# Six of the twelve modulation chunks move from TensorE's four-strip sums to GpSimd and one-column matmuls

## The chip, the cores and the metric

One core of one Trainium2 chip runs the whole program in one launch. The metric is the device time of an execution in microseconds (us). Everything is float32.

## The reference, cut to what matters

One layer of a hybrid diffusion step for 512 sample tokens and 128 prompt tokens, model width 1024. The change touches only where and when the adaLN modulation is computed:

```
cond -> silu(cond) @ w_ada + b_ada            w_ada: 1024 x 6144, two conditions (c, c_ctx)
     -> sh1, sc1, g1, sh2, sc2, g2            six rows of 1024 for each condition
h = rmsnorm(x) * (1 + sc1) + sh1
y = concat(rglru(h ...), hgrn2(h ...)) @ w_out
x = x + g1 * y
h = rmsnorm(x) * (1 + sc2) + sh2
x = x + g2 * expert_choice_ffn(h)             16 experts, capacity 2T/16
```

sh1 and sc1 are wanted at the very start; g1, sh2, sc2 and g2 only after the mixer. A chunk is 512 of the 6144 columns: chunks 0 to 3 are sh1 and sc1 ("early"), chunks 4 to 11 the rest ("late").

## The kernel before, in words

All matrices pass through a ring of six slots in SBUF of 2 MB each (128 partitions, eight k tiles of 512 columns). SyncE issues the loads in the fixed order of LOADS (line 52); each waits until its slot is free (`freed[s]`). The eight late chunks all go through slot 4, one after the other, behind the first projection's weights; then slot 4 takes the weights of the gate projection. Behind them in the same queue stand w_out and the experts' weights (line 345).

Every engine runs an order written out by hand, and the engines meet at semaphores. TensorE's order in the middle of the program: four convolution inputs, the gates of the RG-LRU, five projections of head 0 (HEAD0), one projection taken ahead (EARLY), and then eight "units", one for each of four heads in two directions (line 709). A projection (lines 470 to 489) is eight matmuls of 512 sample columns and eight of 128 prompt columns into one of two PSUM buffers, pa[0] and pa[1], which ScalarE empties; USE numbers them. A unit has two or three projections (FILL) as filler between its own steps: turn v, turn k, the state updates, the scores (five blocks, each masked by VectorE; block n waits for the mask of block n-2), and the outputs. VectorE's side of a unit is: sums of log decays (line 1414), differences (line 1398), weighing of the operands (line 1394), then the state step (lines 1454 to 1463), which writes state_out, and after it the masks (line 1478) and the sum of the outputs.

A modulation chunk (ada_sum, line 491) is eight k steps of four matmuls that have two stationary columns (the two conditions) and 128 moving columns, each of the four in its own strip of 32 PSUM partitions. ScalarE copies two chunks' sums to SBUF, two transposes turn them (ada_turn), and VectorE adds the bias into `mods` (ada_bias). ADA_UNIT says where the pairs of late chunks stand: positions 4 and 5 in unit 0, 6 and 7 in unit 1, 8 and 9 in unit 3, 10 and 11 in unit 5.

GpSimd in this stage only issues DMAs, in order (lines 386 to 402). In unit u it waits for the outputs of unit u-2, loads the state of unit u into s0, then waits for the state step of unit u-1 and stores that state from state_out: the store in iteration u is that of unit u-1, and VectorE's state step of unit u waits for it (line 1457), because it writes the same state_out. Before unit 0 the queue waits for the last RG-LRU state (line 386) and for `lru_y` (line 391).

Of the kernel before, what the change touches and what calls it, by code (L numbers as in the profile page):

```python
# [80 lines left out]
ADA_UNIT = {0: 4, 1: 6, 3: 8, 5: 10}  # L81
# [3 lines left out]
def program(nc, x_prompt, x_sample, state_lru, state_hgrn, c, c_ctx, w_ada, b_ada, norm_mix, w_in,  # L85
# [7 lines left out]
    with ctx:  # L93
# [32 lines left out]
        ada_sb = sb("ada_sb", [P, 2 * P])  # L126
        eps = sb("eps", [P, 1])
# [112 lines left out]
        ada_zero, adr_ps, adr_done = sem("mod_sums_zeroed"), sem("mod_rows_in_psum"), sem("mod_rows_copied")  # L240
        ada_ps, ada_add, mods_done = sem("mods_turned"), sem("mods_added"), sem("mods_done")
# [14 lines left out]
        sp_done = sem("softplus_done")  # L256
# [103 lines left out]
        def _(pool):  # L360
# [24 lines left out]
            pool.dma_start(w_rt[:, :, :], w_router[0].rearrange("(k p) n -> p k n", p=P)).then_inc(s_wbd, 16)  # L385
            pool.wait_ge(lst_done, 1)
            pool.dma_start(flat(new_state_lru).rearrange("(r q) -> r q", q=P), lru_last_r[:, :]).then_inc(st_dma, 16)
            for u in range(2 * HEADS):
                h, d = u // 2, u % 2
                if u == 0:  # L390
                    pool.wait_ge(lru_y, 1)
                if u >= 2:
                    pool.wait_ge(o_ps, u - 1)
                pool.dma_start(s0[u % 2], state_hgrn[0, 0, d, h]).then_inc(s0_in[u % 2], 16)
                if u >= 1:
                    pool.wait_ge(s_done, u)
                    pool.dma_start(new_state_hgrn[0, 0, (u - 1) % 2, (u - 1) // 2], state_out[:, :]).then_inc(st_dma, 16)
                if u == UNITS - 1:
                    pool.wait_ge(rows_cp, 1)
                    pool.dma_start(mod_rows.rearrange("r (k q) -> (r k) q", q=P), row_turn[:, :]).then_inc(rows_st, 16)  # L400
# [54 lines left out]
        def _(pe):  # L455
# [21 lines left out]
            def project_prompt(item):  # L477
                g, j = item
                n, s = USE[item], SLOT_OF[("in", g)][0]
                for k in range(KT):  # L480
                    r = mm(pa[n % 2][:, TS:T], ring[:, s, k, j * P:(j + 1) * P], hT[:, k, TS:T], k == 0, k == KT - 1)
                r.then_inc(full, 1)
# [21 lines left out]
            def ada_turn(at):  # L504
                pe.wait_ge(adr_done, at // 2 + 1)
# [447 lines left out]
        def _(act):  # L953
# [28 lines left out]
            def ada_copy(at):  # L982
# [4 lines left out]
                if at >= 2:  # L987
                    act.wait_ge(ada_ps, at // 2)
# [39 lines left out]
            def lru_gates(j):  # L1028
# [9 lines left out]
                if j == 0:  # L1038
                    act.wait_ge(sp_done, 1)
# [19 lines left out]
            def projected(item):  # L1059
# [3 lines left out]
                src, e = pa[n % 2][:, 0:T], empty[n % 2]  # L1063
                if g == IN_OG:
# [159 lines left out]
        def _(dve):  # L1224
# [38 lines left out]
            def ada_bias(at):  # L1263
                dve.wait_ge(ada_ps, at // 2 + 1)
# [48 lines left out]
            V.tensor_scalar(sp[:, 3, :], acc8, 8.0, None, ALU.mult).then_inc(sp_done, 1)  # L1313
# [94 lines left out]
            for u in range(UNITS):  # L1408
# [42 lines left out]

                if u in ADA_UNIT:
# [221 lines left out]
```

## Time and profile before

| what | us |
|---|---|
| runs of the kernel before | 1067.31, 1068.09, 1062.74; median 1067.31 |
| the profiled execution | 1062.3 |
| its span, first to last instruction | 1060.6 |
| TensorE busy | 992.4 (94%) |
| VectorE busy | 353.8 (33%) |
| ScalarE busy | 288.6 (27%) |
| GpSimd busy | 87.5 (8%), DMA issues almost alone |
| mean granted TensorE clock | 0.98 |

In the rows further down, PE is TensorE, PEld its weight loads, DVE VectorE, ACT ScalarE, POOL GpSimd; SPq and POOLq are the DMA queues of SyncE and GpSimd. L457 is line 457 of the kernel, a helper through which nearly all matmuls pass, so the tiles tell which matmul it is: `ring,cs` is a modulation chunk, `reg_a,ring` a projection. A float32 matmul shows as two records. A timeline row gives its start, the time it covers, and in brackets how long the engine was idle before it and who ended that. The granted clock is 1.00 at TensorE's 2.4 GHz and 0.50 at 1.2 GHz.

### The profile page before, as it was taken

Reading aid. Unit: us, or ns where it says so; the run is one execution under the profiler, and the core shown is the slowest. Engines: PE = TensorE matmul, PEld = TensorE weight load, DVE = VectorE, ACT = ScalarE, POOL = GpSimd, SP = SyncE. Lnnn points to the kernel's source line nnn. Section 1 sums busy time; section 2 is a strip of 40 time slices with the busy share of each in tenths; the row PEclk is TensorE's granted clock in tenths of the full one; section 3 lists DMA queues with packets and bytes.
Section 4 is the critical chain, followed back from the end, with each engine's and each line's share of the span. In section 5 each row is a group of like instructions: output and inputs, shape, how many; then the busy total and the mean of one; then the engine's idle time right before and its main releaser. Section 6 shows DMA issues by size and latency. Waiting matters only on the chain.

```text
span 1060.6 us, 18108 instructions
## 1 busy us (share of the span) xinstructions
PE 992.4 (94%) x7918; PEld 451.8 (43%) x7918; DVE 353.8 (33%) x819; ACT 288.6 (27%) x445; POOL 87.5 (8%) x102
## 2 busy tenths in 40 slices
PE   4999999999999999993999999999999999999990
PEld 3555556666666765553233233333333333333230
DVE  2367726453642663455103021030210302103024
ACT  5147545563652554431100010000100001000012
POOL 2200000000000000000101102011020110201101
PEclk9999999999999999996999999999999999999995
DMA  9980013404028424215499999999999999999947
GB/s 352 353 292 0 1 39 132 164 6 159 6 85 300 185 87 174 80 60 198 159 410 395 399 409 392 404 395 401 410 392 404 393 404 410 393 403 393 404 192 223
DMA packets 82366, 277.26 MB, mean 261 GB/s; under 512 B 3889, under 2 KB 4065, under 8 KB 82321
## 3 DMA queue, kind: packets, MB, share of 16 engines
q1 hardware_dynamic: 74688, 253.24, 61.3%
q0 software_dynamic: 5392, 15.46, 5.3%
q10 hardware_dynamic: 2240, 7.91, 1.9%
q8 instruction: 34, 0.56, 0.2%
q14 instruction: 12, 0.09, 0.0%
HBM read 262.94 MB, written 13.65 MB: 261 GB/s over the span
## 4 chain that ended last, share of the span: by engine, by line
PE 73%; DMA 19%; DVE 4%; SPq 2%; ACT 1%; issue 1%; DVEq 0%; ACTq 0%
PE pa L457 49%; PE p L457 20%; DMA ring<-in_w_up_dram 15%; DMA ring<-in_w_ada_dram 3%; SPq L338 1%; PE p L877 1%; PE p L833 1%; DVE reg_e L1460 1%; DVE reg_a L1647 1%; DMA reg_c<-h_rows,row_s 1%; PE p L838 0%; PE p L594 0%; DMA sum_rows<-reg_c,row_b 0%; PE pa L932 0%; DMA sum_rows<-reg_c,row_s 0%
## 5 line engine op out<-in xcount | busy, mean ns | idle before, releaser
L457 PE MATMUL pa<-ring,reg_b 128*32 128x512 f32 (+1 forms) x3232 | 413.4, 595 | 2.9 <-DMA ring<-in_w_up_dram 2.9
L457 PEld LDWEIGHTS pa<-ring,reg_b 128*32 128x32 f32 (+1 forms) x3232 | 129.9, 114 | 257.3 <-issue 256.8
L457 PE MATMUL pa<-reg_a,ring 128*128 128x128 f32 (+1 forms) x832 | 232.4, 435 | 0.0
L457 PE MATMUL p<-ring,reg_b 128*16 128x512 f32 x1536 | 173.6, 593 | 0.0
L457 PEld LDWEIGHTS pa<-reg_a,ring 128*128 128x128 f32 x832 | 126.1, 191 | 93.6 <-issue 93.6
L963 ACT ACTIVATE reg_b<-pa 128x512 f32<-128x512 f32 (+1 forms) x28 | 17.1, 612 | 284.6 <-PE pa L457 228.7
L1617 DVE TENSOR_TENSOR reg_b<-reg_b,pa 128x512 f32<-128x512 f32 x16 | 11.0, 688 | 247.4 <-PE pa L457 247.4
L457 PEld LDWEIGHTS p<-ring,reg_b 128*16 128x16 f32 x1536 | 43.3, 97 | 112.2 <-issue 108.7
L963 ACT ACT_TABLE_LOAD x64 | 82.1, 1283 | 5.1 <-issue 2.8
L963 ACT ACTIVATE reg_b<-p 128x512 f32<-128x512 f32 x24 | 14.3, 597 | 196.1 <-PE p L877 169.8
L1585 DVE TENSOR_SCALAR reg_b<-p,ffn_scale,mods 128x128 f32<-128x128 f32 x72 | 23.8, 403 | 72.2 <-PE p L833 72.2
L963 ACT ACTIVATE reg_c<-reg_c 128x320 f32<-128x320 f32 (+1 forms) x86 | 43.3, 574 | 1.7 <-DVE reg_c L1377 0.7
L435 POOL DMA_INDIRECT sum_rows<-reg_c,row_s x8 | 11.8, 1471 | 346.5 <-DVE reg_c L1630 346.5
L457 PE MATMUL p<-reg_c 128*16 128x16 f32 (+3 forms) x640 | 36.4, 212 | 2.2 <-DVE reg_e L1478 1.4
L1394 DVE SCALAR_TENSOR_TENSOR reg_c<-reg_c,oml 128x320 f32<-128x320 f32 (+1 forms) x40 | 27.1, 681 | 20.5 <-ACT reg_c L963 20.5
L457 PE MATMUL p<-reg_c,reg_e 128*128 128x128 f32 (+1 forms) x128 | 31.2, 359 | 2.9 <-ACT reg_b L963 1.4
L963 ACT ACTIVATE reg_d<-pa 128x640 f32<-128x640 f32 (+2 forms) x24 | 15.6, 659 | 60.8 <-PE pa L457 60.7
L457 PEld LDWEIGHTS p<-reg_c 128*16 128x16 f32 (+3 forms) x640 | 27.3, 115 | 11.4 <-DVE reg_e L1478 3.0
L1637 DVE SCALAR_TENSOR_TENSOR reg_c<-p,slot_q,reg_c 16x512 f32<-16x512 f32 x32 | 23.9, 746 | 22.8 <-PE p L457 22.4
L1630 DVE SCALAR_TENSOR_TENSOR reg_c<-pa,slot_s,reg_c 128x512 f32<-128x512 f32 x16 | 12.0, 751 | 56.5 <-PE pa L457 56.5
L1398 DVE TENSOR_TENSOR reg_c<-reg_c 128x640 f32<-128x640 f32 x40 | 30.1, 820 | 0.3
L457 PE MATMUL p<-ring,cs 128*2 128x128 f32 x768 | 23.3, 274 | 1.9 <-DMA ring<-in_w_ada_dram 1.8
(248 smaller groups left out, 702.6 us busy)
## 6 DMA issues: line engine op xcount, KB each, us to landing
ring<-in_w_gate_dram SPq DMA_DIRECT2D x32, 2048.0 KB, 14.1
ring<-in_w_up_dram SPq DMA_DIRECT2D x32, 2048.0 KB, 19.0
ring<-in_w_down_dram SPq DMA_DIRECT2D x32, 2048.0 KB, 17.8
ring<-in_w_ada_dram SPq DMA_DIRECT2D x12, 2048.0 KB, 19.5
ring<-in_w_in_dram SPq DMA_DIRECT2D x7, 2048.0 KB, 20.0
ring<-in_w_out_dram SPq DMA_DIRECT2D x2, 2048.0 KB, 16.8
sum_rows<-reg_a ACTq DMA_DIRECT2D x5, 512.0 KB, 2.6
h_rows<-reg_d ACTq DMA_DIRECT2D x5, 512.0 KB, 2.7
```

Source lines behind the costliest of these rows:

```text
L338: sp_eng.dma_start(ring[:, s], src).then_inc(loaded[s], 16)
L435: pool.indirect_dma_start(sum_rows, bass.IndirectOffsetOnAxis(row_s[0:CS, i:i + 1], 0), out_s[0:CS, :], None, compute_op=ALU.add).then_inc ...
L457: return nc.tensor.matmul(out, lhsT, rhs, start=start, stop=stop, **kw)
L833: r = nc.tensor.transpose(p67[:, k * P:(k + 1) * P], xg_s[:, k * P:(k + 1) * P], ident[:, :])
L877: r = nc.tensor.transpose(p67[:, f * P:(f + 1) * P], hid_s[:, f * P:(f + 1) * P], ident[:, :])
L963: return nc.scalar.activation(out, in_, f, **kw)
L1394: return V.scalar_tensor_tensor(dst, src, s, dst, ALU.mult, ALU.mult)
L1398: V.tensor_tensor(dst.rearrange("p (g x) -> p g x", x=x), c3, c3[:, :, at:at + 1].to_broadcast([P, T // x, x]), ALU.subtract).then_inc(sub ...
L1585: r = V.tensor_scalar(xsT[:, k, :], p67[:, k * P:(k + 1) * P], ffn_scale[:, k, 0:1], mods[:, 3 * KT + k, 0:1], ALU.mult, ALU.add)
L1617: V.tensor_tensor(hv, hv, pa[1][:, cols_], ALU.mult).then_inc(hid_done, 1)
L1630: V.scalar_tensor_tensor(out_s[:, cols_], pa[1][:, cols_], slot_s[:, 1, bass.ds(i, 1)], g2r[0][:, cols_], ALU.mult, ALU.mult).then_inc(out ...
L1637: r = V.scalar_tensor_tensor(out_p[32 * e:32 * e + CP, cols_], p45[rs, 512:1024], slot_q[rs, bass.ds(i, 1)], g2r[1][rs, cols_], ALU.mult, ...
```

## The change

Late chunks 4 to 9 (by position) leave TensorE's four-strip sums. For each, GpSimd multiplies the eight k tiles by the condition's value of each partition and adds them up over k, for both conditions, into ada_part (two rows of 512 a partition); of the products, all but the first two are written over ring tiles that are used up. Then eight matmuls with 128 columns of ada_part as weights and one column of ones as the moving operand sum over partitions; they stand at the end of the prompt half of a given projection, and write eight columns of the same PSUM buffer behind it. ADA_AT says which projection: the third of HEAD0, EARLY, and the first fill of units 1, 2, 3 and 4. ScalarE copies the eight columns to ada_cols, and VectorE adds the bias in units 0 (two chunks), 1, 2, 3 and 4. On GpSimd chunks 4 and 5 stand ahead of the store of the last RG-LRU state, and chunks 6 to 9 in iterations 0 to 3 between the load of a state and the store of the last one. GpSimd frees slot 4. Chunks 10 and 11 stay as they were, in unit 5. The semaphore sp_done goes into sp_e.

```diff
--- before.py
+++ after.py
@@ -78,7 +78,13 @@
 N_USE = len(USE)
 UNITS = 2 * HEADS
 
-ADA_UNIT = {0: 4, 1: 6, 3: 8, 5: 10}
+
+ADA_AT = {HEAD0[2]: 4, EARLY: 5, FILL[1][0]: 6, FILL[2][0]: 7, FILL[3][0]: 8, FILL[4][0]: 9}
+
+ADA_UNIT = {5: 10}
+ADA_TURN = {0: 1, 2: 2, 10: 3}
+AT_ITEM = {at: item for item, at in ADA_AT.items()}
+
 Y_ORDER = [4, 5, 6, 0, 1, 2, 3, 7]
 
 
@@ -124,6 +130,8 @@
         ss_h = sb("ss_h", [P, 2, NT])
         z_rt = sb("z_rt", [P, 2, NE])
         ada_sb = sb("ada_sb", [P, 2 * P])
+        ada_part = sb("ada_part", [P, 2, 512])
+        ada_cols = sb("ada_cols", [P, 6, 8])
         eps = sb("eps", [P, 1])
         hn = sb("hn", [P, T])
         cs = sb("cs", [P, KT, 2])
@@ -238,6 +246,7 @@
         pe_cols, pv_done = sem("param_columns"), sem("param_columns_copied")
         cs_done = sem("cond_silu")
         ada_zero, adr_ps, adr_done = sem("mod_sums_zeroed"), sem("mod_rows_in_psum"), sem("mod_rows_copied")
+        part_done = sem("mod_parts_done")
         ada_ps, ada_add, mods_done = sem("mods_turned"), sem("mods_added"), sem("mods_done")
         rows_ps, rows_cp, rows_st = sem("mod_rows_turned"), sem("mod_rows_ready"), sem("mod_rows_stored")
         act_step, dve_step, pool_step = sem("act_step"), sem("dve_step"), sem("pool_step")
@@ -253,7 +262,6 @@
         lru_done, lsq_done = sem("lru_tile_done"), sem("lru_squares")
         ln_ps, ln_log, ln_rstd, lru_y, gr_y = sem("lru_norm_sums"), sem("lru_norm_log"), sem("lru_norm_rstd"), sem("lru_y_done"), sem("lru_y_gated")
         sp_e = sem("softplus_exp")
-        sp_done = sem("softplus_done")
         lfk = sem("logf_and_k")
         qrev = sem("q_v_reversed")
         cum_done, sub_done, exp_done, w_done = sem("cum_done"), sem("decay_diffs"), sem("decay_exps"), sem("unit_operands")
@@ -383,6 +391,40 @@
                         pool.dma_start(wbd[64 * hf:64 * hf + 64, g, d, :, 64 * hf:64 * hf + 64],
                                        src).then_inc(s_wbd, 16)
             pool.dma_start(w_rt[:, :, :], w_router[0].rearrange("(k p) n -> p k n", p=P)).then_inc(s_wbd, 16)
+            pool_steps = [2]
+
+            def chain(ins):
+                pool_steps[0] += 1
+                ins.then_inc(pool_step, 1)
+                pool.wait_ge(pool_step, pool_steps[0])
+
+            def ada_parts(at):
+
+                s, turn = SLOT_OF[("ada", ADA[at])]
+                pool.wait_ge(loaded[s], 16 * (turn + 1))
+                if at == 4:
+                    pool.wait_ge(cs_done, 2)
+                else:
+                    pool.wait_ge(full, USE[AT_ITEM[at - 1]] + 1)
+                for k in range(KT):
+                    w, c0, c1 = ring[:, s, k, :], cs[:, k, 0:1], cs[:, k, 1:2]
+                    if k == 0:
+                        nc.gpsimd.tensor_scalar(ada_part[:, 0, :], w, c0, None, ALU.mult)
+                        chain(nc.gpsimd.tensor_scalar(ada_part[:, 1, :], w, c1, None, ALU.mult))
+                    else:
+                        used = ring[:, s, k - 1, :]
+                        nc.gpsimd.tensor_scalar(used, w, c0, None, ALU.mult)
+                        chain(nc.gpsimd.tensor_scalar(w, w, c1, None, ALU.mult))
+                        nc.gpsimd.tensor_tensor(ada_part[:, 0, :], ada_part[:, 0, :], used, ALU.add)
+                        r = nc.gpsimd.tensor_tensor(ada_part[:, 1, :], ada_part[:, 1, :], w, ALU.add)
+                        if k < KT - 1:
+                            chain(r)
+                r.then_inc(part_done, 1)
+                pool.wait_ge(part_done, at - 3)
+                pool.sem_inc(freed[s], 1)
+
+            ada_parts(4)
+            ada_parts(5)
             pool.wait_ge(lst_done, 1)
             pool.dma_start(flat(new_state_lru).rearrange("(r q) -> r q", q=P), lru_last_r[:, :]).then_inc(st_dma, 16)
             for u in range(2 * HEADS):
@@ -392,6 +434,8 @@
                 if u >= 2:
                     pool.wait_ge(o_ps, u - 1)
                 pool.dma_start(s0[u % 2], state_hgrn[0, 0, d, h]).then_inc(s0_in[u % 2], 16)
+                if u <= 3:
+                    ada_parts(6 + u)
                 if u >= 1:
                     pool.wait_ge(s_done, u)
                     pool.dma_start(new_state_hgrn[0, 0, (u - 1) % 2, (u - 1) // 2], state_out[:, :]).then_inc(st_dma, 16)
@@ -479,6 +523,11 @@
                 n, s = USE[item], SLOT_OF[("in", g)][0]
                 for k in range(KT):
                     r = mm(pa[n % 2][:, TS:T], ring[:, s, k, j * P:(j + 1) * P], hT[:, k, TS:T], k == 0, k == KT - 1)
+                if item in ADA_AT:
+                    pe.wait_ge(part_done, ADA_AT[item] - 3)
+                    for m in range(4):
+                        for c in range(2):
+                            r = mm(pa[n % 2][:, T + 2 * m + c:T + 2 * m + c + 1], ada_part[:, c, m * P:(m + 1) * P], ones[:, 0:1])
                 r.then_inc(full, 1)
                 if j == HEADS - 1:
                     pe.wait_ge(full, n + 1)
@@ -502,7 +551,7 @@
                 r.then_inc(freed[s], 1)
 
             def ada_turn(at):
-                pe.wait_ge(adr_done, at // 2 + 1)
+                pe.wait_ge(adr_done, ADA_TURN[at])
                 for n in range(2):
                     r = nc.tensor.transpose(ada_at(at + n, 1), ada_sb[:, n * P:(n + 1) * P], ident[:, :])
                 r.then_inc(ada_ps, 1)
@@ -985,7 +1034,7 @@
                     s, turn = SLOT_OF[("ada", ADA[at + n])]
                     act.wait_ge(freed[s], turn + 1)
                 if at >= 2:
-                    act.wait_ge(ada_ps, at // 2)
+                    act.wait_ge(ada_ps, ADA_TURN[at] - 1)
                 src = p67[:, 512:768] if at < 4 else p45[:, P:3 * P]
                 A(ada_sb[:, :], src, ACT.Copy).then_inc(adr_done, 1)
 
@@ -1036,7 +1085,7 @@
                         A((rg, ig)[g][b][d], four[2 + n % 2][:, 0:T], ACT.Sigmoid,
                           bias=col(("lru_ba", "lru_bx")[g], 4 * d + j)).then_inc(gate_in, 1)
                 if j == 0:
-                    act.wait_ge(sp_done, 1)
+                    act.wait_ge(sp_e, 5)
                 for d in range(2):
                     act.wait_ge(gate_in, 4 * j + 2 * d + 1)
                     A(th[b][d], rg[b][d], ACT.Tanh, scale=sp[:, 3, 4 * d + j:4 * d + j + 1]).then_inc(gates_done, 1)
@@ -1061,6 +1110,8 @@
                 n = USE[item]
                 act.wait_ge(full, n + 1)
                 src, e = pa[n % 2][:, 0:T], empty[n % 2]
+                if item in ADA_AT:
+                    A(ada_cols[:, ADA_AT[item] - 4, :], pa[n % 2][:, T:T + 8], ACT.Copy)
                 if g == IN_OG:
                     A(yT[:, LT + h, :], src, ACT.Silu).then_inc(e, 1)
                 elif g == IN_GR:
@@ -1261,7 +1312,7 @@
                     modulate(k, buf).then_inc(xt_dve, 1)
 
             def ada_bias(at):
-                dve.wait_ge(ada_ps, at // 2 + 1)
+                dve.wait_ge(ada_ps, ADA_TURN[at])
                 for n in range(2):
                     c = ADA[at + n]
                     V.tensor_tensor(mods[:, 4 * c:4 * c + 4, :], ada_at(at + n, 1).rearrange("p (m x) -> p m x", x=32)[:, :, 0:2],
@@ -1310,7 +1361,7 @@
             chain(V.tensor_tensor(acc8, acc8, sp[:, 5, :], ALU.add))
 
             chain(V.tensor_scalar(sp[:, 4, :], acc8, -8.0, None, ALU.mult))
-            V.tensor_scalar(sp[:, 3, :], acc8, 8.0, None, ALU.mult).then_inc(sp_done, 1)
+            V.tensor_scalar(sp[:, 3, :], acc8, 8.0, None, ALU.mult).then_inc(sp_e, 1)
 
             ada_bias(2)
             dve.wait_ge(ada_add, 4)
@@ -1449,6 +1500,12 @@
                         dve.wait_ge(empty[m % 2], m // 2 + 1)
                         V.tensor_tensor(yT[:, j, :], yT[:, j, :], raw[0][j], ALU.mult).then_inc(gr_y, 1)
 
+                for at in ((4, 5), (6,), (7,), (8,), (9,), (), (), ())[u]:
+                    n = USE[AT_ITEM[at]]
+                    dve.wait_ge(empty[n % 2], n // 2 + 1)
+                    c = ADA[at]
+                    V.tensor_tensor(mods[:, 4 * c:4 * c + 4, :], ada_cols[:, at - 4, :].rearrange("p (m x) -> p m x", x=2),
+                                    bv[:, 4 * c:4 * c + 4].unsqueeze(2).to_broadcast([P, 4, 2]), ALU.add).then_inc(ada_add, 1)
                 if u in ADA_UNIT:
                     ada_bias(ADA_UNIT[u])
                 dve.wait_ge(u_ps, u + 1)
```

## Rows read from the trace of the kernel before

**Rows 1.** Page, the chain of waits by engine, shares of the span.
```profile
PE 73%; DMA 19%; DVE 4%; SPq 2%; ACT 1%; issue 1%; DVEq 0%; ACTq 0%
```

**Rows 2.** Stages: length, busy PE, PEld, DVE, ACT, POOL; clock, DMA share, GB/s.
```profile
78.00:107.00 29.00, 27.15 (x100) 15.00 (x99) 20.69 (x30) 22.78 (x28) 0.00 (x0) 1.00 0.00 1
176.30:206.50 30.20, 30.07 (x312) 20.12 (x311) 15.09 (x32) 15.71 (x28) 1.08 (x2) 1.00 0.42 145
460.00:1030.00 570.00, 550.45 (x4909) 181.45 (x4911) 109.77 (x290) 52.99 (x78) 57.00 (x48) 0.98 0.93 363
```

**Rows 3.** Timeline of TensorE: start, time covered, line, out<-in, records.
```profile
107.03 17.47 PE L457 MATMUL pa<-reg_a,ring 128*128 128x512 f32 x64
...
144.88 1.25 PE L457 MATMUL p<-reg_c,ones 128*128 128x512 f32 x4
...
169.54 4.68 PE L457 MATMUL p<-reg_c 128*128 128x128 f32 x80
...
183.22 1.93 PE L457 MATMUL p<-ring,cs 128*2 128x128 f32 x64
185.08 2.05 PE L457 MATMUL pa<-reg_a,ring 128*128 128x128 f32 x16
186.97 0.71 PE L594 MATMUL p<-ident,reg_d 128*128 128x128 f32 x5
...
198.62 0.38 PE L507 MATMUL p<-ident,ada_sb 128*128 128x128 f32 x2
198.83 1.06 PE L457 MATMUL p<-reg_e,reg_c 128*128 128x128 f32 x8
...
206.45 7.03 PE L457 MATMUL pa<-reg_a,ring 128*128 128x512 f32 x16
...
216.18 0.71 PE L594 MATMUL p<-ident,reg_d 128*128 128x128 f32 x5
...
244.15 0.71 PE L594 MATMUL p<-ident,reg_d 128*128 128x128 f32 x5
```

**Rows 4.** Timeline of TensorE, unit 6: the router bias.
```profile
351.51 3.64 PE L457 MATMUL p<-w_rt,mods 128*128 128x16 f32 x32
```

**Rows 5.** Timeline of VectorE: last weighing of unit 0, state steps of units 1, 2, 3.
```profile
150.04 3.27 DVE L1389 SCALAR_TENSOR_TENSOR reg_b<-reg_c,pv,reg_d 128x640 f32<-128x640 f32 x4 [3.48 <-ACT reg_d L963]
...
167.11 1.22 DVE L1394 SCALAR_TENSOR_TENSOR reg_c<-reg_d,reg_c 128x320 f32<-128x320 f32 x2
...
199.93 1.11 DVE L1460 SCALAR_TENSOR_TENSOR reg_e<-reg_e,decay,p 128x128 f32<-128x128 f32 x3 [0.66 <-PE p L457]
...
226.91 1.11 DVE L1460 SCALAR_TENSOR_TENSOR reg_e<-reg_e,decay,p 128x128 f32<-128x128 f32 x3 [1.34 <-PE p L457]
...
265.80 1.12 DVE L1460 SCALAR_TENSOR_TENSOR reg_e<-reg_e,decay,p 128x128 f32<-128x128 f32 x3 [0.66 <-PE p L457]
```

**Rows 6.** Groups of GpSimd's instructions: busy us, mean ns of one, idle before.
```profile
L372 POOL MEMSET reg_e<- 128x2048 f32 x1 | 1.8, 1801 | 0.0
...
L365 POOL TENSOR_SCALAR_AFFINE_SELECT ident<-ident 128x128 f32<-128x128 f32 x1 | 0.3, 282 | 0.1
L363 POOL MEMSET ones<- 128x128 f32 x1 | 0.2, 210 | 0.0
```

**Rows 7.** SyncE's loads through slot 4, ring loads' times to landing, the state stores.
```profile
68.47 241.04 SPq L338 DMA_DIRECT2D ring<-in_w_ada_dram  x8
...
DMA to landing us min/median/max: 7.7/18.6/26.8
...
out_dram<-state_out POOLq DMA_DIRECT2D x8, 64.0 KB, 3.2
```

**Rows 8.** Router logits in two places, and the stage table behind a gap.
```profile
468.64 1.85 PE L457 MATMUL p<-w_rs,reg_d 128*128 128x16 f32 x16
...
500.00 3.53 PE L457 MATMUL pa<-w_rs,reg_d 128*128 128x16 f32 x16 [2.88 <-ACT reg_d L963]
...
504.00:506.00 2.00, 2.00 (x12) 0.40 (x8) 0.57 (x4) 1.44 (x3) 0.00 (x0) 0.50 0.00 0
```

## The prediction

> **What bounds the kernel now.** I read first the chain of waits [rows 1]: TensorE holds 73% of it, DMA 19%. Then the stage table [rows 2]: in the third stage shown, the loop over the experts, DMA engines are 93% used at 363 GB/s, so that loop takes its time from whenever it starts. In the second, unit 1 of the mixer, TensorE is busy for 30.07 of 30.20 us. The six chunks are all computed in front of or inside those units, while TensorE has no gap. So every microsecond put on or taken from TensorE there moves the expert loop by the same, and the end with it. Then the timeline of TensorE [rows 3], to see each chunk's price and the times at which things are needed; then VectorE [rows 5] and GpSimd [rows 6].
>
> **What goes.** A chunk on TensorE is 64 records that start at 183.22 and are done when the next work starts at 185.08 [rows 3]: 1.86 us, since four column strips run side by side. Two transposes per pair of chunks: 198.62 to 198.83, 0.21. Unit 0 loses two chunks and a pair of transposes, 3.9 us; unit 1 and unit 3 the same. In all 11.8 us.
>
> **What comes on TensorE.** Eight matmuls a chunk with 128x128 weights and one moving column. The nearest row is the router bias [rows 4]: 128x128 weights, 16 moving columns, 32 records (two a matmul) in 3.6 us, 0.225 us a matmul. A matmul with 128 columns costs hardly more (16 records, 8 matmuls, 1.9 us between 185.08 and 186.97 in [rows 3]), so the weights set the price, not the columns, and one column cannot be much cheaper. I take 0.225: 1.8 us a chunk, 10.8 in all; zero is the other end. **So TensorE's own account is -1.0 us**: the work left it in name only. ScalarE's extra copies of 128x8 stand behind a projection in a second buffer; nobody waits.
>
> **Unit 0 gives part of it back.** VectorE ends the operands of the scores at 167.11 + 1.22 = 168.3 [rows 5]; TensorE starts the scores at 169.54 [rows 3]. The cover is 1.2 us, and VectorE's chain starts from the norm behind the last pre-unit projection, which no removed sum precedes. With 3.9 us gone from TensorE it waits 2.7. Net so far +1.8 us.
>
> **What comes on GpSimd.** Per chunk 16 tensor_scalar and 14 tensor_tensor on 128x512, 15 waits on itself and one at the end. The trace of before has neither operation. GpSimd rows are fills: 1.80 us for 2048 elements and 0.21 for 128, so 0.83 ns an element plus 0.1, or 0.53 us for 512; a select that also reads takes 0.28 against the fill's 0.21 at 128 [rows 6]. Lower end: each costs a fill, 30 x 0.53 = 16 us. Upper end: every operand pass takes a fill's rate one after the other, 0.95 for one input and 1.38 for two, 34.5 us plus 16 waits of 0.1, 36. Taken: the select's extra per element (0.07 / 128 x 512 = 0.28) partly kept, 0.75 for one input; one more pass for the second, 1.15; 12.0 + 16.1 + 1.6 = 30 us a chunk (T). I lean to the upper half because two inputs have to be read.
> The Trainium skill (GPSIMD Engine Reference, section 3.1) gives 4497 ns for a two-input add of 2048 elements; a quarter is 1.12 us, by which estimate T would be some 28. No row here shows it.
>
> **Where T meets the path.** Three orders matter. (a) A chunk is needed at the end of a given projection. (b) Chunk n+1 may start only when the projection that uses chunk n is done (one ada_part buffer) and its load has landed in slot 4, freed by chunk n. (c) GpSimd's queue is in order: in units 1, 2 and 3 the store of the last unit's state now stands behind a whole chunk. VectorE's state step waits for that store, and the masks, the last three score blocks and the outputs stand behind the state step. In the rows of before GpSimd did nothing between, so the store was out long before.
> - Chunk 4: load issued at 68.5 and landed 7.7 later at best [rows 7], 76.2 to 106.2; needed when the first of the two projections starting at 107.03 ends, 8.7 later at 115.7 [rows 3]. Hidden, cover 9.5; past that every us is paid.
> - Chunk 5: 117.5 to 147.5. Needed at 144.9 + 1.8 = 146.7: 0.8 late. Unit 0 starts 4.4 late.
> - Chunk 6: starts after lru_y (153.3 + 4.4, [rows 5]) and 0.6 for a state load, 158.3 to 188.3. Unit 0 ends 3.2 late (4.4 - 3.9 + 2.7), unit 1 starts at 179.5, its first projection ends 186.97 - 176.3 (unit 1's start, [rows 2]) - 1.86 = 8.8 later at 188.3: just in time. With the one-column matmuls 190.1.
> - Unit 1, chunk 7: slot 4 was freed at 188.3, load landed 196.0, chunk to 226.0, store landed 3.2 later [rows 7], 229.2. The state step [rows 5] would have been at 199.93 + 3.2 - 3.9 + 1.8 = 201.0. Stall 28.2. From the state step to the unit's end is 6.5 (199.93 to 206.45).
> - After such a stop TensorE's clock is low: at 504 to 506, behind the gap that ends at 500.00, the granted clock is 0.50 (the 1.2 GHz level) and the same 16 logit records take 3.53 us instead of 1.85 [rows 8]. Six us at half speed cost 3.0 a stall. Unit 1 ends at 238.7, 32.3 late.
> - Unit 2, chunk 8: the first projection ends 9.73 (206.45 to 216.18, [rows 3]) + 1.8 into the unit, 250.2; chunk to 280.2, store 283.4; natural 226.91 + 32.3 + 1.8 = 261.0. Stall 22.4. Ends 59.5 late with the clock.
> - Unit 3, chunk 9: the first projection ends 244.15 - 233.4 - 1.86 + 1.8 = 10.7 into the unit, 303.6; to 333.6, store 336.8; natural 265.80 + 59.5 - 2.1 = 323.2. Stall 13.6. Ends 74.0 late.
> - Unit 4 has only the one-column matmuls, +1.8: 75.8.
> Units 5 to 7, the output projection and the experts follow unchanged: the last two chunks stay on TensorE, GpSimd is free, and the expert weights that could be loaded early wait for slots that unit 5 frees. 1062.3 (the profiled execution, span 1060.6) + 75.8 = **1138 us**. That execution is 5 us under the median 1067.31 and inside the runs' 1062.74 to 1068.09; against the median the same sum gives 1143. I take 1140.
>
> **The rivals.**
> - *Cheap GpSimd, T of 16 to 23.* For: the fills. At 16: unit 1's chunk runs 189.3 to 205.3, store 208.5 against 200.2, stall 8.3; unit 2 8.4; unit 3 none; with two clock penalties and the other terms +24.5, so 1087. At 23 the stalls are about 15, 15 and 7, near 1110.
> - *The two engines take turns.* VectorE's instructions of this stage nearly all read two SBUF tensors, and it is busy 20.7 of 29 us in the first stage and 15.1 of 30.2 in unit 1 [rows 2]. If one waits for the other for whole instructions, a chunk grows by the VectorE work in its window: about 8 in each of units 1 to 3 (+24), 15 for chunk 5, and unit 0's operands (some 20 instructions, each held by nearly a GpSimd instruction) come 17 later, while chunk 4's 9.5 of cover goes too, some +3. 75.8 + 59: about 1197. Against it: no GpSimd computation runs beside VectorE in the trace of before, so the rows can't say.
>  The Trainium skill (SBUF — State Buffer, "Who interferes with whom") says that a VectorE instruction with two SBUF inputs and a GpSimd instruction that reads SBUF exclude each other for the whole instruction. That is this rival, with no run here yet beside it.
> - *Not slower.* The state store never decides: needs T + 3.2 under the 10.8 us between the first projection with its matmuls and unit 2's state step, T under 7.6, 0.25 us an instruction. Then +1.8 less what cheaper one-column matmuls give (up to 10.8 if free): 1053 to 1065. Against it: half of the cheapest fill of that size.
>
> **How the numbers follow.** Forecast case (T 24 to 35, engines apart or nearly: 1115 to 1160) 0.48; turns (1160 to 1205) 0.26; cheap GpSimd 0.18; not slower 0.04; beyond 1205, 0.04. The range 1090 to 1195 leaves out the ends of the second and third and the last two. About 0.5% is what can be told from no change here. Slower 0.96, same 0.025, faster 0.015.
>
> **What would show it.** In the changed trace: GpSimd near full from 76 us to the end of unit 3, T read from one chunk's first to last instruction; TensorE idle before the third score block or the outputs in units 1, 2, 3 with VectorE's state step released by the state_out transfer; one-column matmuls at 0.2 us each; the granted clock at 0.5 after each stop; the expert loop as long as before. VectorE instructions far over 0.82 us beside GpSimd show the turns. I am wrong if T is under 20, if the stores leave before the chunk ends, or if the pre-unit stage already loses more than a few us.

## The result, and the profile after

The changed kernel takes 1261.93 us (median of 4 runs, 1258.67 to 1264.46) where the kernel before takes 1067.24 (1062.74 to 1068.09): a ratio of 1.184, 95% interval 1.180 to 1.187. The prediction was 1140 us, between 1090 and 1195. The sign was right, and the places where TensorE stops are the ones named; the size was not: 195 us were lost where the prediction's sum had 75.8. In the runs further down, one of the twelve executions of the kernel with short chunks took 2672.3 us, more than twice its others, and is left out of its ratio.

First the page of the changed kernel: span, then busy us of each engine (share of the span) and instructions.

```profile
span 1259.5 us, 17709 instructions
PE 1022.1 (81%) x7624; PEld 474.2 (38%) x7624; DVE 386.1 (31%) x819; ACT 289.1 (23%) x448; POOL 364.6 (29%) x282
```

GpSimd went from 87.5 to 364.6 us. VectorE has as many instructions as before (819) and is busy 32 us longer. TensorE has 1 us less to do by the forecast account and is busy 30 us longer: the granted clock is 0.90 in place of 0.98, and behind a stop the same records take longer (48 score records 4.39 us where the kernel before has 2.78). At the end of unit 3 TensorE is 188.8 us later than before (461.15 against 272.33), in unit 7 it is 198.4 later and at the end of the span 198.9: what follows the mixer only shifts.

Now GpSimd's groups in the changed kernel (busy us, mean ns of one, idle before). These are the operations for which [rows 6] had only fills.

```profile
L416 POOL TENSOR_SCALAR ring<-ring,cs 128x512 f32<-128x512 f32 x42 | 74.1, 1764 | 4.1
L417 POOL TENSOR_SCALAR ring<-ring,cs 128x512 f32<-128x512 f32 x42 | 69.2, 1648 | 0.0
L419 POOL TENSOR_TENSOR ada_part<-ada_part,ring 128x512 f32<-128x512 f32 x42 | 58.1, 1384 | 0.0
L418 POOL TENSOR_TENSOR ada_part<-ada_part,ring 128x512 f32<-128x512 f32 x42 | 56.3, 1340 | 3.5
```

And one k step of chunk 5 while VectorE stands idle (timeline: start, duration). The starts show the undisturbed price better than the means.

```profile
153.74 1.56 POOL L416 TENSOR_SCALAR ring<-ring,cs 128x512 f32<-128x512 f32 x1
155.28 1.56 POOL L417 TENSOR_SCALAR ring<-ring,cs 128x512 f32<-128x512 f32 x1
156.92 1.27 POOL L418 TENSOR_TENSOR ada_part<-ada_part,ring 128x512 f32<-128x512 f32 x1
158.15 1.27 POOL L419 TENSOR_TENSOR ada_part<-ada_part,ring 128x512 f32<-128x512 f32 x1
159.52 1.56 POOL L416 TENSOR_SCALAR ring<-ring,cs 128x512 f32<-128x512 f32 x1
```

A k step is 5.78 us (153.74 to 159.52), so an undisturbed chunk is 7 x 5.78 + 3.2 = 43.7 us, and the six took 52.3, 46.2, 50, 44.4, 45.5 and 45.9.

Where TensorE stood still for long, in the timeline of the changed kernel (in brackets the idle time and who ended it):

```profile
105.15 6.58 PE L501 MATMUL p<-reg_c,reg_e 128*128 128x512 f32 x16 [7.80 <-ACT reg_c L1012]
115.63 4.12 PE L501 MATMUL p<-reg_c,reg_e 128*128 128x512 f32 x8 [3.90 <-ACT reg_b L1012]
...
182.52 3.57 PE L501 MATMUL pa<-ones,ada_part 128*128 128x1 f32 x16 [23.12 <-POOL ada_part L419]
...
245.66 3.58 PE L501 MATMUL pa<-ones,ada_part 128*128 128x1 f32 x16 [14.45 <-POOL ada_part L419]
...
307.49 4.39 PE L501 MATMUL p<-reg_c 128*128 128x128 f32 x48 [44.42 <-DVE reg_e L1535]
...
380.30 4.39 PE L501 MATMUL p<-reg_c 128*128 128x128 f32 x48 [41.64 <-DVE reg_e L1535]
...
453.29 4.39 PE L501 MATMUL p<-reg_c 128*128 128x128 f32 x48 [33.15 <-DVE reg_e L1535]
```

Two kinds of stop. At 182.5 and 245.7 a projection waits for its chunk. At 307, 380 and 453 (units 1, 2, 3) TensorE has done two score blocks and waits for VectorE's mask. What VectorE waited for in unit 1 is one step further back; here are GpSimd's store and VectorE's state step, which answers to the one at 199.93 in [rows 5]:

```profile
300.08 0.60 POOL L441 DMA_DIRECT2D out_dram<-state_out  x1 [0.62 <-POOL ada_part L419]
```
```profile
305.79 1.12 DVE L1517 SCALAR_TENSOR_TENSOR reg_e<-reg_e,decay,p 128x128 f32<-128x128 f32 x3 [46.35 <-DMA out_dram<-state_out]
```

The store leaves when the chunk ends (its idle time is ended by `ada_part`), and 5.7 us later its landing ends 46 us of VectorE's waiting: order (c) of the prediction, chunk, store, state step, masks, scores. Order (b), a chunk that waits for the load into the slot which the last chunk freed, stands in GpSimd's timeline at the start of chunk 5, and the load that is let go when chunk 7 ends stands in SyncE's:

```profile
136.31 1.74 POOL L412 TENSOR_SCALAR ada_part<-ring,cs 128x512 f32<-128x512 f32 x1 [8.35 <-DMA ring<-in_w_ada_dram]
```
```profile
299.53 0.37 SPq L346 DMA_DIRECT2D ring<-in_w_ada_dram  x1
```

The stage table of the changed kernel around that stop (window, length, busy us of PE, PEld, DVE, ACT, POOL; granted clock):

```profile
264.00:306.00 42.00, 0.00 (x0) 0.00 (x0) 0.21 (x1) 0.00 (x0) 35.50 (x27) 0.52 0.13 44
306.00:313.00 7.00, 5.51 (x53) 4.38 (x54) 2.42 (x9) 0.00 (x0) 0.00 (x0) 0.50 0.16 59
```

For 42 us TensorE issued nothing, and the next 7 us of work ran at 0.50, the 1.2 GHz level. The clock also dipped where no stop had been forecast and none is seen. Here are the stage table of unit 6, and a filler projection in it (7.11 us for the same records in the kernel before, at a granted clock of 1.00):

```profile
550.00:562.00 12.00, 12.00 (x35) 6.44 (x36) 5.52 (x12) 5.21 (x9) 0.00 (x0) 0.74 0.00 0
```
```profile
550.62 9.88 PE L501 MATMUL pa<-reg_a,ring 128*128 128x512 f32 x16
```

The one-column matmuls at full clock cost what was forecast: 16 records from 128.24, the next work at 129.94, 1.70 us a chunk (1.8 forecast).

### The profile page after: what moved, and what is told of

It reads as the page before. It is cut to its first block and busy times, and to the rows that moved or that the text cites. A ratio compares the mean times of both kernels' runs of the same rounds, so it can differ in the third digit from the quotient of the medians.

```text
span 1259.5 us, 17709 instructions
## 1 busy us (share of the span) xinstructions
PE 1022.1 (81%) x7624; PEld 474.2 (38%) x7624; DVE 386.1 (31%) x819; ACT 289.1 (23%) x448; POOL 364.6 (29%) x282
## 5 line engine op out<-in xcount | busy, mean ns | idle before, releaser
L501 PE MATMUL pa<-reg_a,ring 128*128 128x128 f32 (+1 forms) x832 | 240.3, 446 | 0.0
L501 PEld LDWEIGHTS pa<-reg_a,ring 128*128 128x128 f32 x832 | 131.1, 198 | 98.6 <-issue 98.5
L501 PE MATMUL p<-reg_c 128*16 128x16 f32 (+3 forms) x640 | 42.5, 228 | 121.7 <-DVE reg_e L1535 121.4
L479 POOL DMA_INDIRECT sum_rows<-reg_c,row_s x8 | 11.8, 1478 | 344.9 <-DVE reg_c L1687 344.9
L1012 ACT ACTIVATE reg_b<-pa 128x512 f32<-128x512 f32 (+1 forms) x28 | 17.2, 613 | 285.4 <-PE pa L501 229.5
L501 PEld LDWEIGHTS p<-reg_c 128*16 128x16 f32 (+3 forms) x640 | 31.6, 128 | 132.6 <-DVE reg_e L1535 122.5
L416 POOL TENSOR_SCALAR ring<-ring,cs 128x512 f32<-128x512 f32 x42 | 74.1, 1764 | 4.1
L417 POOL TENSOR_SCALAR ring<-ring,cs 128x512 f32<-128x512 f32 x42 | 69.2, 1648 | 0.0
L419 POOL TENSOR_TENSOR ada_part<-ada_part,ring 128x512 f32<-128x512 f32 x42 | 58.1, 1384 | 0.0
L418 POOL TENSOR_TENSOR ada_part<-ada_part,ring 128x512 f32<-128x512 f32 x42 | 56.3, 1340 | 3.5
L1012 ACT ACTIVATE reg_c<-reg_d 128x640 f32<-128x640 f32 (+2 forms) x24 | 12.5, 553 | 175.3 <-PE p L501 173.0
L1517 DVE SCALAR_TENSOR_TENSOR reg_e<-reg_e,decay,p 128x128 f32<-128x128 f32 x24 | 8.3, 347 | 143.4 <-DMA out_dram<-state_out 128.5
L501 PE MATMUL p<-reg_c,reg_e 128*128 128x128 f32 (+1 forms) x128 | 37.8, 418 | 12.7 <-ACT reg_c L1012 7.8
L1642 DVE TENSOR_SCALAR reg_b<-p,ffn_scale,mods 128x128 f32<-128x128 f32 x72 | 23.8, 405 | 72.3 <-PE p L882 72.3
L501 PE MATMUL pa<-ones,ada_part 128*128 128x1 f32 x96 | 14.5, 281 | 37.6 <-POOL ada_part L419 37.6
## 6 DMA issues: line engine op xcount, KB each, us to landing
ring<-in_w_down_dram SPq DMA_DIRECT2D x32, 2048.0 KB, 15.7
```

What stands on the lines that cost most here:

```text
L416: nc.gpsimd.tensor_scalar(used, w, c0, None, ALU.mult)
L417: chain(nc.gpsimd.tensor_scalar(w, w, c1, None, ALU.mult))
L418: nc.gpsimd.tensor_tensor(ada_part[:, 0, :], ada_part[:, 0, :], used, ALU.add)
L419: r = nc.gpsimd.tensor_tensor(ada_part[:, 1, :], ada_part[:, 1, :], w, ALU.add)
L479: pool.indirect_dma_start(sum_rows, bass.IndirectOffsetOnAxis(row_s[0:CS, i:i + 1], 0), out_s[0:CS, :], None, compute_op=ALU.add).then_inc ...
L501: return nc.tensor.matmul(out, lhsT, rhs, start=start, stop=stop, **kw)
```

## The experiments

### TensorE's own account: chunks cut to their first k step

```diff
-                for k in range(KT):
+                for k in range(1):
```

> The changed kernel with each GpSimd chunk cut to its first k step (two products; the sums over the other seven k tiles are left out), everything else in its place: 8 one-column matmuls a chunk, the copies, the buffer and queue orders. GpSimd's chunk falls from 44.7 us (undisturbed) to 3.2 us. Theory A (the length of a GpSimd chunk, carried to TensorE by three orders, is the whole loss; TensorE's own account is near nil): 1060 to 1068 us, no waits of TensorE on ada_part, granted clock back at 0.98. Rival B (what the chunks bring on TensorE, ScalarE and in the queues costs by itself): above 1075 us.

1070.4 us; ratio to the runs of before 1.0035, interval 1.0016 to 1.0054, so +2 to +6 us. That lies between theory A's 1060 to 1068 and rival B's 1075, and much nearer to A. TensorE's waits on GpSimd are gone:

```profile
115.39 1.84 PE L501 MATMUL pa<-ones,ada_part 128*128 128x1 f32 x16
...
168.76 1.09 PE L650 MATMUL p<-ident,reg_c 128*128 128x128 f32 x4 [3.17 <-ACT reg_e L1012]
```

No one-column matmul waits. 6 x 1.70 = 10.2 us came, 11.8 went, and unit 0 waits 3.2: +1.6, near the forecast +1.8. One part of it was off: the 3.2 us are at the turning of k and are ended by ScalarE's copy of v, not at the scores by VectorE's operands. So nearly the whole loss of the change comes with the length of GpSimd's chunks, and with chunks of hardly any length it still isn't faster than before.

### The order of the queue: store ahead of the chunk

```diff
-                if u <= 3:
-                    ada_parts(6 + u)
                 if u >= 1:
                     pool.wait_ge(s_done, u)
                     pool.dma_start(new_state_hgrn[...], state_out[:, :]).then_inc(st_dma, 16)
+                if u <= 3:
+                    ada_parts(6 + u)
```

> The changed kernel with the chunk of iteration u of GpSimd's queue put behind the store of the last unit's state, not ahead of it. Theory A (that order costs, beside the length): the state steps of units 1 to 3 no longer wait; in their place TensorE waits for the chunk at the first projection of units 2 to 4, each now one chunk plus one slot-4 load (44.7 + 8.3 us) behind the last. By hand unit 4 ends near 428 us where it ends near 498 now: about 1190 us. Rival B (GpSimd's total work is the bound whatever the order): 1250 to 1262 us.

1214.6 us (ratio 1.139, 1.136 to 1.142), 47 less than the change. TensorE's long stops are all of the first kind now:

```profile
247.54 3.58 PE L501 MATMUL pa<-ones,ada_part 128*128 128x1 f32 x16 [11.68 <-POOL ada_part L419]
306.71 3.57 PE L501 MATMUL pa<-ones,ada_part 128*128 128x1 f32 x16 [25.70 <-POOL ada_part L419]
360.75 3.57 PE L501 MATMUL pa<-ones,ada_part 128*128 128x1 f32 x16 [22.23 <-POOL ada_part L419]
419.68 3.57 PE L501 MATMUL pa<-ones,ada_part 128*128 128x1 f32 x16 [17.10 <-POOL ada_part L419]
```

That is theory A's picture, with less gained than its 1190. Chunks now run beside VectorE's work and not beside its waiting: the last three take 49.7, 45.6 and 49.1 us where the changed kernel has 44.4, 45.5 and 45.9, and the steps from one to the next are 54 to 59 us and not 53. That is 13 of the 25 us missed. Unit 4 ends at 443.1 us and not near 428, and some 9 us more come behind it; those no run explains.

### The length alone: without the additions

```diff
                         nc.gpsimd.tensor_scalar(used, w, c0, None, ALU.mult)
-                        chain(nc.gpsimd.tensor_scalar(w, w, c1, None, ALU.mult))
-                        nc.gpsimd.tensor_tensor(ada_part[:, 0, :], ada_part[:, 0, :], used, ALU.add)
-                        r = nc.gpsimd.tensor_tensor(ada_part[:, 1, :], ada_part[:, 1, :], w, ALU.add)
+                        r = nc.gpsimd.tensor_scalar(w, w, c1, None, ALU.mult)
```

> The changed kernel without GpSimd's additions (all 16 products of a chunk are made, the 14 adds are left out). A chunk is 8 x (1.56 + 1.54 + 0.1) = 25.6 us undisturbed. Theory A (the recorded working was right but for the length of a chunk, the landing of the store at 5.6 us and some 4.5 us of low clock a stop): the same chain of sums gives 1132 us. Rival B (VectorE and GpSimd take turns, and that carries the loss, since every product reads SBUF too): 1150 us and more.

1151.6 us (ratio 1.080, 1.077 to 1.083). By the trace the chunks took 33.4, 30.0, 29.0, 27.6, 27.6 and 27.4 us, not 25.6 (the products beside VectorE took up to 2.7 us each). This is about the length that the prediction assumed (30), and the time is 12 to 14 us above its 1138 to 1140. Fed with these six lengths the recorded chain of sums gives 1130, and the profiled execution took 1153.3: the chain is right in its main part and some 24 us short in others. By the numbers written down for this run theory A (1132) is missed by 20 us and rival B's 1150 and more is met. The time alone can't say whether turns are the cause that B names; the fills further down put them at 18 of the 195 us in the changed kernel, where they don't carry the loss.

### The kind of operation: products by tensor_tensor

```diff
-                        nc.gpsimd.tensor_scalar(used, w, c0, None, ALU.mult)
+                        nc.gpsimd.tensor_tensor(used, w, c0, ALU.mult)      # c0, c1 broadcast to 512 columns
```

> The changed kernel with the products made by tensor_tensor against the condition's value broadcast along the row, not by tensor_scalar with a pointer scalar. In the changed kernel a tensor_tensor starts 1.23 us after the one before it and a tensor_scalar 1.55. Theory A (the operation's kind sets its price): all 30 at 1.23, a chunk of 38.7 us in place of 44.7, and 5 of 6 chunks on the path: about 1230 us. Rival B (the price is in reading two operands or a broadcast): no gain, 1255 us and more.

1234.1 us (ratio 1.156, 1.152 to 1.159). A product is now cheaper than an add:

```profile
229.30 1.04 POOL L416 TENSOR_TENSOR ring<-ring,cs 128x512 f32<-128x512 f32 x1
230.30 1.04 POOL L417 TENSOR_TENSOR ring<-ring,cs 128x512 f32<-128x512 f32 x1
231.42 1.27 POOL L418 TENSOR_TENSOR ada_part<-ada_part,ring 128x512 f32<-128x512 f32 x1
```

1.00 us against 1.55: an undisturbed chunk would be 16 x 1.00 + 14 x 1.23 + 1.6 = 35 us, 9 less. Six times 9 is 54 and only 28 came. In the trace the chunks took 46.9, 42.7, 40.9, 38.0, 38.7 and 38.0 us, in sum 39 less than in the changed kernel. VectorE paid too: its busy time rose from 386.1 to 432.2 us, TensorE's two waits on ScalarE in the pre-unit stage grew from 7.8 and 3.9 to 13.5 and 4.3, and TensorE waits 6.1 us for VectorE's operands in unit 0. The total met the expectation by luck: the price per product was lower than expected, and the loss to VectorE was not in the expectation at all.

### Who holds whom: three probes in the kernel before

GpSimd works on scratch that nobody waits for, beside VectorE's first RG-LRU half; with a kind of instruction each.

```diff
+            pool.wait_ge(gates_done, 4)
+            for _ in range(14):                  # tensor: 18, fill: 40
+                chain(nc.gpsimd.tensor_scalar(b, a, cs[:, 0, 0:1], None, ALU.mult))
+                                                 # tensor: tensor_tensor(b, a, a, ALU.add); fill: memset(b, 0.0)
+            pool.wait_ge(sc_zero, 1)             # VectorE idle: three more, and others
```

> The kernel before, and 14 GpSimd tensor_scalar instructions of 128x512 with a pointer scalar on scratch that nobody waits for, beside VectorE's first RG-LRU half (83 to 103 us, 24 instructions that read two SBUF tensors); then, while VectorE is idle from 132 us on, three more, and two with an immediate scalar. Theory A (whole-instruction turns between VectorE instructions with two SBUF inputs and GpSimd instructions that read SBUF): the VectorE instructions grow by up to one GpSimd instruction each, its busy time from 83 us on goes from 20 to 35 us or more. Rival B (they share, partly): less than 10 us more. Either way the time is within 15 us of 1067. With an immediate scalar: 0.6 to 1.2 us if the pointer is what makes tensor_scalar dearer than tensor_tensor, 1.55 if not.

> As the probe before, with 18 tensor_tensor adds of 128x512 on GpSimd in place of the 14 tensor_scalar, and three adds and three copies while VectorE is idle. Theory A (turns): VectorE's busy time grows as beside tensor_scalar. Rival B (the share of the time in which GpSimd reads decides): more than beside tensor_scalar, since two operands are read in 1.23 us in place of one in 1.55. Time within 15 us of 1067.

> As the probes before, with 40 fills of 128x512 on GpSimd (which read nothing), and three while VectorE is idle. Theory A (only GpSimd instructions that read SBUF meet VectorE's second input): VectorE's instructions keep 0.82 us at 640 elements and the time stays at 1062 to 1068. Rival B (any GpSimd instruction that uses SBUF does): they grow as beside tensor_scalar. A fill undisturbed: 0.53 us, as the fills of the kernel before say.

Single runs: 1069.5, 1075.9 and 1067.3 us, beside one run of the kernel before of 1061.8. VectorE's timeline is the measurement; by the pages its busy time is 357.2, 366.7 and 354.6 us (353.8 in the kernel before). The same instructions in the kernel before:

```profile
83.16 0.83 DVE L1358 TENSOR_TENSOR reg_d<-reg_c 128x640 f32<-128x640 f32 x1 [8.18 <-ACT reg_c L963]
83.90 0.82 DVE L1358 TENSOR_TENSOR hn<-reg_c 128x640 f32<-128x640 f32 x1
84.75 0.83 DVE L1361 SCALAR_TENSOR_TENSOR reg_c<-reg_d,reg_c 128x640 f32<-128x640 f32 x1
85.50 0.82 DVE L1361 SCALAR_TENSOR_TENSOR reg_c<-hn,reg_c 128x640 f32<-128x640 f32 x1
```

beside tensor_scalar,

```profile
83.21 1.06 DVE L1386 TENSOR_TENSOR reg_d<-reg_c 128x640 f32<-128x640 f32 x1 [8.18 <-ACT reg_c L991]
84.20 0.81 DVE L1386 TENSOR_TENSOR hn<-reg_c 128x640 f32<-128x640 f32 x1
85.04 1.20 DVE L1389 SCALAR_TENSOR_TENSOR reg_c<-reg_d,reg_c 128x640 f32<-128x640 f32 x1
86.16 0.81 DVE L1389 SCALAR_TENSOR_TENSOR reg_c<-hn,reg_c 128x640 f32<-128x640 f32 x1
```

beside tensor_tensor,

```profile
82.61 0.83 DVE L1386 TENSOR_TENSOR reg_d<-reg_c 128x640 f32<-128x640 f32 x1 [8.18 <-ACT reg_c L991]
83.36 1.66 DVE L1386 TENSOR_TENSOR hn<-reg_c 128x640 f32<-128x640 f32 x1
85.05 1.54 DVE L1389 SCALAR_TENSOR_TENSOR reg_c<-reg_d,reg_c 128x640 f32<-128x640 f32 x1
86.52 1.66 DVE L1389 SCALAR_TENSOR_TENSOR reg_c<-hn,reg_c 128x640 f32<-128x640 f32 x1
```

and beside fills,

```profile
84.52 0.82 DVE L1389 SCALAR_TENSOR_TENSOR reg_c<-reg_d,reg_c 128x640 f32<-128x640 f32 x1
```

The whole half, first instruction to the last before the next wait, takes 21.1 us before, 21.1 beside fills, 23.8 beside tensor_scalar and 33.2 beside tensor_tensor (some of its last instructions run free again). On GpSimd's side, probes beside VectorE and with VectorE idle:

```profile
81.23 30.41 POOL L397 TENSOR_SCALAR scr<-scr,cs 128x512 f32<-128x512 f32 x14 [46.78 <-ACT reg_b L991]
134.23 4.88 POOL L397 TENSOR_SCALAR scr<-scr,cs 128x512 f32<-128x512 f32 x3 [22.59 <-DVE reg_e L1412]
139.19 3.06 POOL L399 TENSOR_SCALAR scr<-scr 128x512 f32<-128x512 f32 x2
```
```profile
80.59 27.18 POOL L401 TENSOR_TENSOR scr<-scr 128x512 f32<-128x512 f32 x18 [46.27 <-ACT reg_b L991]
144.00 3.28 POOL L401 TENSOR_TENSOR scr<-scr 128x512 f32<-128x512 f32 x3 [36.23 <-DVE reg_e L1412]
147.34 1.96 POOL L403 COPY scr<-scr 128x512 f32<-128x512 f32 x3
```

A tensor_scalar goes from 1.63 to 2.17 us, a tensor_tensor from 1.09 to 1.51. (These prices hold the wait after each instruction; the probe's add reads one tile twice, where the add in the changed kernel, at 1.23, reads two.) With an immediate scalar (2 in 3.06) it costs 1.53: the pointer is not what makes it dear. A copy is 0.65. So of the tensor_scalar theories the partial one (B) holds, beside tensor_tensor VectorE's time grows more, as rival B of the second probe has it (the reason that it gives, the share of reading, is not shown by that), and fills leave VectorE alone (A of the third). The same pattern stands in the changed kernel: up to 1.90 us where an add runs beside, 0.81 to 1.20 where a tensor_scalar runs alone beside. The Trainium skill (SBUF — State Buffer, "Who interferes with whom") has the two exclude each other for a whole instruction when VectorE has two SBUF inputs and GpSimd reads. Fills agree with it, tensor_tensor nearly (a whole instruction of waiting would make 0.82 + 1.09 = 1.91 us, and 1.66 is measured); beside tensor_scalar the rows don't: VectorE's instructions hardly grow while a 2.17 us one runs, and it is GpSimd that pays.

### As long, but reading nothing

```diff
-                for k in range(KT):
+                for k in range(1):
 ...
+                for n in range(13):
+                    r = nc.gpsimd.memset(ring[:, s, 1:KT, :], 0.0)
+                    if n < 12:
+                        chain(r)
```

> The changed kernel with GpSimd's work on k tiles 1 to 7 replaced by 13 fills of 128x3584, which read nothing and last as long (the sums over those tiles are left out): a chunk of some 44.5 us that leaves VectorE alone. Theory A (length and orders are the bulk, the two engines' meeting at SBUF the rest): the waits of TensorE on ScalarE at 105 and 115 us fall back to 1.1 and 0.7, chunks 4 and 6 are 7.6 and 5.4 us shorter, in sum 17 us less than the changed kernel, 1244 us. Rival B (the meeting carries the loss): under 1200 us. Rival C (nothing of it is the meeting, GpSimd is just slow): 1258 to 1265 us.

1243.5 us (ratio 1.166, 1.162 to 1.169), 1244 expected. VectorE is back at 355.4 us of busy time and TensorE's waits in the pre-unit stage at what they were before, while the long stops stay:

```profile
99.04 4.72 PE L505 MATMUL p<-reg_c,reg_e 128*128 128x512 f32 x16 [1.14 <-ACT reg_c L1016]
...
172.93 3.57 PE L505 MATMUL pa<-ones,ada_part 128*128 128x1 f32 x16 [18.03 <-POOL ring L423]
...
229.99 3.58 PE L505 MATMUL pa<-ones,ada_part 128*128 128x1 f32 x16 [13.79 <-POOL ring L423]
...
292.54 4.39 PE L505 MATMUL p<-reg_c 128*128 128x128 f32 x48 [45.37 <-DVE reg_e L1539]
365.86 4.39 PE L505 MATMUL p<-reg_c 128*128 128x128 f32 x48 [41.07 <-DVE reg_e L1539]
436.12 4.39 PE L505 MATMUL p<-reg_c 128*128 128x128 f32 x48 [31.23 <-DVE reg_e L1539]
```

The chunks took 44.0, 44.3, 44.0, 45.3, 45.0 and 44.0 us, so chunks 4 and 6 are 8.3 and 6.1 shorter than in the changed kernel (7.6 and 5.4 expected). In this change the meeting of the two engines is worth 1261.9 - 1243.5 = 18 us; the other 177 are length, orders, clock and the few us that the kernel with short chunks kept.

### Both mends together

The store ahead of the chunk and the tensor_tensor products.

> Store ahead of the chunk and tensor_tensor products together. Alone the first gave 1214.6 and the second 1234.1 where the change has 1261.9. Theory A (they add up, since one shortens the chunk and the other takes the store off it): 1180 to 1190 us, still far above the 1067 of the kernel before, because six chunks of 35 us and six loads of slot 4 between them are longer than the stage. Rival B (with the store off the path the contention with VectorE takes over): 1200 us and more.

1170.8 us (ratio 1.099, 1.095 to 1.103): better than the sum of the two alone (47 + 28 = 75; 91 came) and than theory A's 1180 to 1190, and still 104 us above the kernel before. Its stops on chunks are 13.6, 1.1, 18.4 and 6.5 us, where the store alone put ahead left 4.3, 19.8, 11.7, 25.7, 22.2 and 17.1; why the two do more together was not taken apart. No run tried a second ada_part buffer or another ring slot, so what orders (a) and (b) cost each by itself is not known. No run pointed to a form of this change that beats it: the form with nearly free chunks stood at 1.0035.

## Why the prediction was wrong

**What held.** TensorE's account (-1.0 us forecast; 10.2 against 11.8, so -1.6). The size of the give-back in unit 0 (2.7; 3.2 measured), though by luck: the wait is another one than forecast. The three orders, each seen as a stop in its place, and the store that waits behind a chunk, which the second experiment took away. The low clock behind each stop. That the expert loop only shifts. (Its side estimate of some 28 us for T comes out at 29.3 by its own sum; nothing else used it.)

**What failed: T, the length of a GpSimd chunk, the "Taken" step.** It was put at 30 us, with 36 as the upper end; undisturbed it is 43.7. Of its two prices, 1.15 us for two inputs was close (1.23). The price for one input, 0.75, is 1.55 in truth, above the "upper end" of 0.95 too. The mistake is in the reasoning: the bounds counted passes over operands at a fill's rate, and took for granted that an instruction that reads less costs less. Here the one-input arithmetic is dearer than the two-input one, and than a copy at 0.65; neither of them could be read off a fill. An upper end built from the only rows at hand was no upper end.

With T = 44.6 (between the undisturbed 43.7 and the 45.3 that the last three chunks took on average; the chunks of fills, which leave VectorE alone, took 44.4 on average), the recorded chain of sums gives chunk 5 ending 21 us late instead of 0.8, chunk 6 15 us late instead of just in time, and stops of 43, 37 and 28 us in units 1 to 3: 1216 us. That is 78 of the 123 us between the 1138 of the sum and the 1261.4 of the profiled execution. The rest, as estimates: 7 from the store, 2.4 more in each of three units (below); 18 from the meeting with VectorE (shown by the fills); 12 that are left of the lag at the end of unit 3, where five stops and not three pull the clock down; and 8 in units 4 to 6, where the lag grows from 188.8 to 198.4 us and only 1.8 was forecast, with granted clocks of 0.74 to 0.86 in stretches in which TensorE hardly waits (1.00 in the same stretches of the kernel before). What sets those off stays open; no run separates the last two shares. The two runs with chunks of known length agree: fed with its own lengths, the chain is 24 us short of the kernel without additions (1130 against 1153.3) and 28 of the one with fills (1215 against 1243.0).

**The rival of turns** was real and mis-sized. It was priced at 59 us with whole-instruction waits on both sides; at the true length it is 18. It had 18 of them for chunks 4 and 5, 17 in unit 0 and 24 in units 1 to 3. Against the fills, the changed kernel is 9.6 us late at the end of chunk 5's projection (182.52 against 172.93), 15.7 at chunk 6's (245.66 against 229.99) and 17.2 at the stop of unit 3 (453.29 against 436.12). So most of it falls up to the first projection of unit 1, and after that units 1 to 3 add 1.5 us where 24 were priced, because VectorE is standing still waiting for the store while GpSimd works.

**The store's landing** was taken from the median of all state stores, 3.2 us [rows 7]. The range behind that median is 1.8 to 5.5. In the changed kernel it was 5.6, 5.7 and 5.5 us in units 1 to 3, where it counted. The chunk's end frees slot 4, and the 2 MB load that this lets go (299.53) is issued just ahead of the 64 KB store (300.08). That this company is what slows the store is likely and not shown by a run of its own; the change itself made the slow case the usual one.

**The range.** 1195 was the case of the forecast T plus turns. A longer T alone passes it: 14.6 us more of T are 78 us of time by the chain, over five for one, because every chunk but the first stands on the path whole, and of the first what is past its 9.5 us of cover. That made T the term to be widest on.

## What to carry to other kernels

Work moved to an idle engine is priced by its length on that engine before its absence on the other: six chunks of 1.9 us became six of 44, in front of a stage that lasts 30 a unit. Ask which later instruction of the same queue somebody waits for; here a 64 KB store. And where the only rows of an operation's engine are of another kind, an upper bound from them isn't one: where every microsecond of T counts over five times, the range has to be as wide as the ignorance of T.

## What the runs showed of the hardware that was not expected

- GpSimd's tensor_scalar on 128x512 float32 starts 1.55 us after the one before it, pointer or immediate scalar alike (1.53), a tensor_tensor add 1.23, a tensor_tensor against a broadcast column 1.00, a copy 0.65, a fill 0.58 with a wait. The Trainium skill (GPSIMD Engine Reference, section 4.1) has GpSimd's one-input operations roughly at line rate and its two-input ones about twice as slow as VectorE's. VectorE's two-input instruction takes 0.82 us for 640 elements, so some 0.66 for 512 by an estimate: the copy and the add agree, the tensor_scalar, 2.3 times as long, does not.
- VectorE's two-input instructions double beside GpSimd's tensor_tensor (0.82 to 1.66 us) and grow little beside its tensor_scalar, which is itself held up (1.63 to 2.17). Beside fills nothing changes.
- A one-column float32 matmul with 128x128 weights takes 0.21 us (eight in 1.70), hardly less than one of 128 columns at 0.24 (eight in 1.89, [rows 3]).
- With tensor_tensor products GpSimd's chunk is shorter (38.0 to 46.9 us against 44.4 to 52.3) and VectorE is busy 46 us longer (386.1 to 432.2).
